# Startup of a two-block transformer kernel: loads reordered, the filter's last products moved behind the start of the first projection pass, adaLN units dealt one to three per pass

## The reference, cut to what matters

```python
mod_l = split(silu(c) @ ada_w + ada_b, 6)          # adaLN: shift, scale, gate (twice)
mod_c = split(silu(c_ctx) @ ada_w + ada_b, 6)
zc = modulate(rmsnorm(ctx, norm1_w), mod_c[0], mod_c[1]) @ w_in + b_in
zl = modulate(rmsnorm(x, norm1_w), mod_l[0], mod_l[1]) @ w_in + b_in
# hyena filter: features -> sin -> sin -> third layer, times a decay
h = sin(freq * (feats @ w1 + b1)); h = sin(freq * (h @ w2 + b2))
h = (h @ w3).reshape(L, 2, 2, 512) * exp(-t * abs(hy_decay))
kf = rfft(two_sided(h) / norm)                     # used by the hyena branch
# mLSTM branch (q, k, v, o), Fourier branch (fn), hyena branch (vh, x1, x2)
x = x + mod_l[2] * merge(gates, branches) @ w_out
x = x + mod_l[5] * hier_moe(...)
```

## Time and profile before

| | |
|---|---|
| runs | 2058.23, 2065.55, 2066.7 us; median 2065.55 |
| profiled execution | 2061.8 us, of which span 2060.0 |
| TensorE busy | 93% of the span |
| startup (to the first projection product) | 62.8 us |
| ten passes | 62.8 to 305 us |
| merge of the branches and `w_out` | to about 420 us |

### The profile page before, as it was taken

The page is one execution under the profiler, slowest core; times in us unless marked ns, Lnnn a source line. Parts: engine busy times, 40 slices in busy tenths (PEclk is TensorE's granted clock), DMA queues, the critical chain, the costliest instruction groups (busy, mean ns, idle before and its releaser), DMA issues.

```text
span 2060.0 us, 45934 instructions
## 1 busy us (share of the span) xinstructions
PE 1916.1 (93%) x20794; PEld 1295.1 (63%) x20794; DVE 663.8 (32%) x1618; ACT 295.3 (14%) x668; POOL 15.5 (1%) x25
## 2 busy tenths in 40 slices
PE   5999999998899698899997997799999999999997
PEld 2664878885795356477775555466666666666665
DVE  2656674522212455322323453301101101110123
ACT  2212121001111224100001133101000000100001
POOL 0100000000000000000000000000000000000000
PEclk7999999999899898899998998899999999999999
DMA  9856763236797422367675240499999999999995
GB/s 362 284 205 236 253 223 114 95 105 197 251 347 284 175 98 82 118 211 243 213 261 184 98 143 17 170 368 387 399 386 402 387 395 395 389 401 393 399 386 209
DMA packets 225611, 528.55 MB, mean 257 GB/s; under 512 B 14960, under 2 KB 72656, under 8 KB 225088
## 3 DMA queue, kind: packets, MB, share of 16 engines
q1 hardware_dynamic: 221168, 509.17, 67.2%
q0 software_dynamic: 1984, 8.79, 1.2%
q10 hardware_dynamic: 2256, 7.56, 1.0%
HBM read 520.49 MB, written 4.98 MB: 255 GB/s over the span
## 4 chain that ended last, share of the span: by engine, by line
PE 86%; DVE 8%; ACT 2%; DMA 2%; issue 1%; DVEq 1%; SPq 0%; ACTq 0%
PE ps L1164 26%; PE ps L1176 13%; PE ps L1120 8%; PE ps L1335 7%; PE ps L793 5%; PE ps L1102 4%; PE ps L986 4%; DVE ring L1910 3%; PE ps L1187 2%; PE ps L1001 2%; PE ps L666 2%; DMA ring<-in_ada_w 1%; PE ps L1382 1%; PE ps L688 1%; PE ps L1409 1%
## 5 line engine op out<-in xcount | busy, mean ns | idle before, releaser
L1164 PE MATMUL ps<-ring,arena 128*32 128x256 f32 (+1 forms) x10752 | 547.8, 364 | 3.8 <-DVE dn L2470 3.1
L1164 PEld LDWEIGHTS ps<-ring,arena 128*32 128x32 f32 x10752 | 364.5, 110 | 179.2 <-DVE dn L2470 3.3
L1176 PE MATMUL ps<-ring,arena 128*32 128x256 f32 x4992 | 276.0, 379 | 2.9 <-DVE arena L2527 2.9
L1176 PEld LDWEIGHTS ps<-ring,arena 128*32 128x32 f32 x4992 | 169.4, 110 | 103.4 <-issue 4.2
L1120 PE MATMUL ps<-hT,ring 128*128 128x256 f32 x704 | 158.2, 386 | 9.9 <-DMA ring<-in_w_ff_down 9.9
L2513 DVE TENSOR_TENSOR arena<-arena,ps 128x256 f32<-128x256 f32 (+1 forms) x72 | 26.9, 373 | 400.0 <-ACT arena L1720 400.0
L1335 PE MATMUL ps<-ring,hT 128*128 128x512 f32 (+1 forms) x384 | 153.6, 553 | 1.0 <-DVE hT L1939 1.0
L1120 PEld LDWEIGHTS ps<-hT,ring 128*128 128x128 f32 x704 | 135.5, 194 | 28.6 <-DMA ring<-in_w_ff_down 10.0
L1335 PEld LDWEIGHTS ps<-ring,hT 128*128 128x128 f32 x384 | 70.5, 191 | 70.2 <-issue 69.8
L1910 DVE SCALAR_TENSOR_TENSOR ring<-ring,cact 128x512 f32<-128x512 f32 x133 | 99.9, 751 | 10.3 <-issue 0.4
L793 PE MATMUL ps<-hT,ring 128*128 128x256 f32 x384 | 90.7, 390 | 2.1 <-DVE hT L1939 2.1
(11 more groups left out here) (386 smaller groups left out, 1648.7 us busy)
## 6 DMA issues: line engine op xcount, KB each, us to landing
ring<-in_w_exp_down SPq DMA_DIRECT2D x176, 512.0 KB, 7.9
ring<-in_w_exp_gate SPq DMA_DIRECT2D x128, 512.0 KB, 5.4
ring<-in_w_exp_up SPq DMA_DIRECT2D x128, 512.0 KB, 7.1
ring<-in_w_ada SPq DMA_DIRECT2D x48, 768.0 KB, 6.2
ring<-in_w_in SPq DMA_DIRECT2D x36, 768.0 KB, 7.4
ring<-in_w_exp_gate SPq DMA_DIRECT2D x64, 384.0 KB, 6.4
ring<-in_w_exp_up SPq DMA_DIRECT2D x64, 384.0 KB, 8.3
ring<-in_ada_w SPq DMA_DIRECT2D x24, 768.0 KB, 8.2
```

The source lines that it names most:

```text
L1164: last = mm(ps[32 * q:32 * q + 32, base + t_, j * n:(j + 1) * n], src[:, k, 32 * t_:32 * t_ + 32], w[:, q], start=k == 0 and j == 0, stop= ...
L1176: last = mm(ps[32 * q:32 * q + 32, bank + t_ // 2, (t_ % 2) * 256:(t_ % 2 + 1) * 256], rows[:, t_, o:o + 32], cells[:, cell, r * D + q * 2 ...
```

## The change

It does four things.

1. ScalarE's queue no longer loads ctx and the `cs`/`ss` tables; GpSimd's queue does, after the rows of units 0 to 3 (`strip_mm` 4). The decay is loaded as one row of 8 KB, and TensorE spreads it to 128 partitions: 4 products of a row of ones with 512 values each, ahead of unit 0. ScalarE takes the absolute value from PSUM. The other tables (2.3 MB) load only in the second pass.
2. The third filter layer moves into pass q: half of it after piece 0, half after piece 2. VectorE's products with the exponentials follow there, with ctx's norm between; ScalarE's exponentials come after `hT`. `turn("ctx")` waits for them. Unit 3's columns come after `turn("x1")`.
3. The adaLN units are dealt by `PASS_ADA`: one in each of the first three passes, two in v, vc and o, three in vh, x1 and x2, two in fn (before: two in each). `SUMMED` is renumbered; still seven units.
4. The filter's norms move one place back in pass k (`norm_of_filters` after piece 2), and its last step on VectorE one convolution forward.

```diff
-SUMMED = (10, 11, 12, 13, 14, 17, 19)
+PASS_ADA = (4, 5, 6, 7, 9, 11, 13, 16, 19, 22, 24)
+SUMMED = (7, 8, 9, 10, 11, 15, 18)
...
-        a, b = ADA_UNITS[4 + 2 * p:6 + 2 * p]
+        group = ADA_UNITS[PASS_ADA[p]:PASS_ADA[p + 1]]
         unit = ("in1", IN1_UNIT[name])
-        loads = loads + ([unit] if unit not in loads else []) + [a, b]
-        releases = releases + [a] + ([unit] if name not in ("k", "v") else []) + [b]
+        early = group if len(group) == 1 else group[:-1]
+        loads = loads + ([unit] if unit not in loads else []) + group
+        releases = releases + early + ([unit] if name not in ("k", "v") else []) + group[len(early):]
...
-            pool.dma_start(region(R_DEC, 2048), A["hy_decay"][0].rearrange("o d c -> (o d c)").partition_broadcast(P)
-                           ).then_inc(sem("decay_in"), 16)
-            pool.wait_ge(sem("strip_mm"), 2)
-            pool.dma_start(blob[:, NFILTER:NCONST], blob_in[:, NFILTER:NCONST]).then_inc(sem("consts_in"), 16)
-            pool.wait_ge(sem("filter_mm"), 6)
+            pool.dma_start(region(R_DEC, 2048)[0:1], A["hy_decay"].rearrange("a o d c -> a (o d c)")).then_inc(sem("decay_in"), 16)
+            pool.wait_ge(sem("strip_mm"), 4)
+            pool.dma_start(late[:, :].rearrange("p (b d) -> p b d", b=NT),
+                           A["ctx"][0].rearrange("(b p) d -> p b d", p=P)).then_inc(sem("ctx_in"), 16)
+            pool.dma_start(blob[:, NEARLY:NFILTER], blob_in[:, NEARLY:NFILTER]).then_inc(sem("spectra_tables_in"), 16)
+            pool.wait_ge(sem("filter_mm"), 7)
...
+            pool.wait_ge(sem("half_mm"), 2)
+            pool.dma_start(blob[:, NFILTER:NCONST], blob_in[:, NFILTER:NCONST]).then_inc(sem("consts_in"), 16)
...
             pe.wait_ge(sem("ident_in"), 16)
+            pe.wait_ge(sem("decay_in"), 16)
+            for j in range(4):
+                last = mm(ps[:, 4 + j, :], const("ones")[0:1, :], region(R_DEC, 2048)[0:1, j * 512:(j + 1) * 512],
+                          start=True, stop=True)
+            last.then_inc(sem("filter_mm"), 1)
...
-            strip_rows(1)
-            strip_columns(1)
-            pe.wait_ge(sem("filter_h"), 2)
-            pe.wait_ge(sem("w3_in"), 16)
-            filter_rows(0, 0, 0)
-            filter_rows(0, 1, 4)
-            strip_rows(2)
-            filter_rows(1, 0, 6)
-            strip_columns(2)
-            pe.wait_ge(sem("filter_h3"), 1)
-            filter_rows(1, 1, 0)
+            for i in (1, 2):
+                strip_rows(i)
+                strip_columns(i)
             strip_rows(3)
-            strip_columns(3)
-            pe.wait_ge(sem("filter_h3"), 3)
...
+            pe.wait_ge(sem("decay"), 1)
             turn("x1")
+            strip_columns(3)
...
+            def with_filter_rows(i):
+
+                if i == 0:
+                    pe.wait_ge(sem("filter_h"), 2)
+                    pe.wait_ge(sem("w3_in"), 16)
+                    filter_rows(0, 0, 4)
+                    filter_rows(0, 1, 6)
+                elif i == 2:
+                    pe.wait_ge(sem("filter_h3"), 2)
+                    filter_rows(1, 0, 4)
+                    filter_rows(1, 1, 6)
...
-            in_pass(0, nothing)
+            in_pass(0, with_filter_rows)
+            pe.wait_ge(sem("filter_h3"), 4)
             turn("ctx")
```

More of the change, by code:

```diff
@@ L765, in bank_free @@
                 else:
-                    pe.wait_ge(sem("filter_h3"), 4)
+                    pe.wait_ge(sem("filter_a"), 2)
             def source(p):
@@ L1552, in _ @@
             sqrt_of(1, 2, st[:, 0:2], std)
+            strip_in(1)
             act.wait_ge(sem("filter_a"), 2)
             ac(fc, fa, ACT.Sin).then_inc(sem("filter_h"), 1)
[L1555 to L1561 removed]
+            act.wait_ge(sem("filter_mm"), 2)
+            ac(region(R_DEC, 2048), all_ps[:, 2048:4096], ACT.Abs).then_inc(sem("decay"), 1)
             strip_in(2)
@@ L1589, in ml_exp @@
                 ac(w, w, ACT.Exp).then_inc(sem("ml_exp"), 1)
+            act.drain()
+            for b in range(NT):
+                ac(region(R_EXP + 2048 * b, 2048), region(R_DEC, 2048), ACT.Exp, scale=const("tneg")[:, b:b + 1]).then_inc(sem("decay"), 1)
+            act.drain()
             strip_in(4)
             z_in("q", 0)
+            sqrt_of(2, 2, st[:, 0:2], std)
+            z_in("q", 1)
+            turned(2, hTc, gac, modc)
+            strip_in(5)
             act.wait_ge(sem("filter_pq"), 1)
@@ L2052, in _, with filters_in @@
             norm_columns(1, hT, ga, mod)
+            def filters_in(b):
+                for o in range(2):
+                    bank = 4 + 2 * o
+                    dve.wait_ge(sem("filter_mm"), 4 + 2 * b + o)
+                    dve.wait_ge(sem("decay"), b + 2)
+                    v.tensor_tensor(h3[:, b, o, :, :].rearrange("p d n -> p (d n)"), ps[:, bank:bank + 2, :].rearrange("p a n -> p (a n)"),
+                                    region(R_EXP + 2048 * b + 1024 * o, 1024), ALU.mult).then_inc(sem("filter_h3"), 1)
+            filters_in(0)
+            dve.wait_ge(sem("ctx_in"), 16)
+            norm_rows(2, late[:, :].rearrange("p (b d) -> p b d", b=NT))
+            filters_in(1)
+            fence()
+            v.memset(h3[0:1, 0, :, 1, :], 0.0)
+            fence()
             for o in range(2):
@@ L2057, in _ @@
             last.then_inc(sem("filter_pq"), 1)
-            dve.wait_ge(sem("ctx_in"), 16)
-            norm_rows(2, late[:, :].rearrange("p (b d) -> p b d", b=NT))
             fence()
```

79 lines of the change are left out of this document (30 added, 49 removed).

## The result

The changed kernel took 2076.86 us (median of 8 executions, 2071.71 to 2081.99), the kernel before on the same chip 2064.77 (8 executions, 2058.23 to 2068.25): ratio 1.0066, 95% interval 1.0046 to 1.0086. It is slower by two thirds of a per cent, where 0.3% faster was forecast; the range ended at 2066. The profiled execution took 2081.2 us.

The account below looks back on a forecast made before the run. TensorE was taken as the bound, with slack only in startup waits and half clock before pass q. Terms 18.3-7.3-0.8-3.3-1.9=5.0 us gave 2056.8 from 2061.8; forecast median 2058.5, range 2050 to 2066.

Parts of the forecast that it names:

- Startup: Before pass q: fewer early loads start its first piece at 44.5 us instead of 62.76; gain 18.3, bounds 15.3 and 22.2.
- the spreading: Ahead of unit 0's rows: four decay products, 7.12 us at half clock, free if `filter` lands by 7.4 us.
- the fast bound: Startup at 2.4 GHz, bound by loads: pass q starts at 40.6 us, a gain of 22.2.
- Third layer: Third filter layer moved into pass q: costs 7.3 us at full clock, bounds 7.3 and 14.5.
- Pass v: TensorE's wait for VectorE in pass v grows from 1.6 to 2.4 us, costing 0.8.
- the sum: All terms up to the merge: 18.3-7.3-0.8-3.3-1.9=5.0 us gained, subtracted from 2061.8.
- Merge wait: Behind pass fn: merge 0, released later, lands at 313.9 us, wanted at 310.56; 3.3 us of new wait.
- slow `gates_of(0)`: Behind the merge wait: TensorE falls to half clock, costing 1.9 us, bounds 0 and 1.9.
- Whatever starts pass q earlier shifts everything after it: From pass q on: an earlier start moves all later work, because TensorE's progress releases later loads.
- Rival D: Pass q and ctx's transposes: the clock doesn't come back after the `hT` wait, 26.3 us more, 2083; chance 0.08.

Follow-up runs that it names:

- before_again: The kernel before, run once more unaltered: 2064.26 us (ratio 0.9984).
- after_two: The changed kernel with its third part undone (two units in every pass, old `SUMMED`): 2057.41 us (ratio 0.9977).
- after_shift: The changed kernel with the first piece of pass fn computed twice: 2067.84 us (ratio 0.9999).
- before_shift: The kernel before with the first piece of pass fn computed twice: 2078.28 us (ratio 1.0061).
- before_nudge: The kernel before with extra 128x256 products ahead of pass fn's first piece: six, 2076.73 us (1.0049); four, 2074.68 us (1.0036).
- after_late: The changed kernel with the first eight products of the second attention's projections computed twice: 2080.62 us (ratio 1.0070).
- after_nudge2: The changed kernel with two extra 128x256 products ahead of pass fn's first piece: 2079.46 us (ratio 1.0052).
- two_nudge6: The changed kernel with part 3 undone and six extra 128x256 products in pass fn: 2069.07 us (ratio 1.0020).
- after_att4: The changed kernel with four extra 128x256 products ahead of the second attention's third projection: 2076.12 us (ratio 1.0045).
- before_att1: The kernel before with one extra 128x256 product ahead of the second attention's third projection: 2069.48 us (ratio 1.0004).
- the fill: Unread 128x128 products in the waits of both attentions' tails; added to the changed kernel: 2066.62 us (ratio 1.0000).
- parts 1 and 2 with the fill: The changed kernel with part 3 undone, plus unread 128x128 products in the waits of both attentions' tails: 2057.89 us (ratio 0.9952).

## Why the prediction was wrong

**Startup: right, against a late base.** The first piece starts at 41.71 us against 44.5 forecast, a gain of 21.05, inside the bounds of 15.3 to 22.2. But the base of 62.76 was one execution's, the latest of five: before_again has 55.78, with 17 us at half clock where the first profile had 31. By the means of five the gain is 17.3. Unit 3's rows start at 32.29, behind a DMA wait (31.9 forecast). `filter` landed at 8.74 and not at 7, so the spreading (7.19 us, forecast 7.1) ended at 16.97 and unit 0's rows began at 16.90 instead of 15.7; the DMA waits behind absorbed that. TensorE was back at full clock for most rows between; that and the late base brought the result near the fast bound.

By the Trainium skill (DMA: Bandwidth & Descriptors, Queues, rings and completion order: each engine takes turns between queues), a queue less brings `filter` forward. It did, from 11.12 to 8.74, but by less than I took it for; no run shows the turns.

**Third layer: right.** 3.70+3.70=7.40 us at full clock, forecast 7.3. A wait of 1.07 for unit 4, on which nothing was counted, came in front.

**Pass v: right in the wait, short in the clock.** 2.48 us against 1.6 before, forecast 2.4. The columns and the spectrum behind it took 1.87+6.05 against 1.33+4.95 before: 1.6 us more that the sum left out. These terms give 21.05-7.40-1.07-0.88-1.64=10.1 where 12.40 us were measured at the end of pass fn; most of the rest is a half-clock stretch that the kernel before had at 203 us (clock 0.98 from 200 to 290 us, worth 1.8 us) and the changed kernel has not (1.00).

**Merge wait: right mechanism, too small.** 4.64 us, forecast 3.3, and 2.82 for the slow `gates_of(0)`, forecast 1.9; merge 0 is issued from 290.79 us on and lands at 302.75, 12.0 us later where 10.7 were reckoned from release to landing, while `fnet_columns` ends at 294.47+3.69=298.16. after_two shows both terms by their absence, 7.57 us. What came out larger on either side cancels: 4.78 behind the merge, forecast 5.0. That the sum met the measured pair is luck: the cancelling terms, and the base again, since the five profiles of each kernel have 0.8.

**The step that failed** is "Whatever starts pass q earlier shifts everything after it", taken to the end: the sum of 5.0 was subtracted from 2061.8 as if the identical stages behind the merge kept their durations. They didn't; 24 us were lost there in the profiled pair, of which 3.7 came without a lower clock, and by the medians some 13 (12.1 us between them and a mean lead of 0.8). The smaller failure is the base: one execution's 62.76 stood for the kernel, and the lead of 5.0 was 0.8 on average. Rival D named the right mechanism, a clock that doesn't come back, and its 2083 us was nearer than the forecast, but it sat in pass q, where the clock was 1.00 from 46 to 72 us. No row from behind 320 us went into the sum, since the change doesn't touch those stages, and so it left out that the two attentions already stood at a granted clock of 0.85 and 0.89.

**What is shown and what stays open.** Shown: that most of the loss is half-clock time in unchanged stages (stretches, rows, and the clock of every execution); that it isn't a remnant of the change (after_shift removes most of it, before_shift and the two before_nudge kernels bring a loss into the kernel before); that in the 18 profiles without a fill the long stretch goes with the place of the fall in the attention's work, though this was read off 14 of them, and 0.04 us separate the last fall with it from the first without; that with the waits filled no execution's mean clock is under 0.967, the highest of all the others. Only argued: that the place of the fall is the cause of the long stretch, and that the changed kernel's median lies high because its earlier stages bring it to the bad place oftener. Two profiles against two, and the medians, speak for it, but the forecasts by offset (after_late, after_nudge2, two_nudge6, after_att4, before_att1) failed, and I can't say which kernel will meet it. Why the changed kernel has more half-clock time than the kernel before thus stays open. Open also: whether the fill works by less idle time or because it is plain products. The tail is rich in transposes. The Trainium skill (TensorE: Matmul & The Clock Gate, Part 4) says that transposes don't count as activity in the same way; no run here separates the two. The Trainium skill (TensorE: Matmul & The Clock Gate, HAM oscillation) ties falls to single long waits between bursts. The trace has them with none longer than 1.95 us just ahead, so a long wait isn't needed for a fall here; whether several short ones are what brings it, no run separates.

## What to carry to other kernels

Where TensorE waits often between small products, its clock is on a knife's edge, and any edit upstream, even one that saves time, can tip it: look at the granted clock of all stages before costing a change, and count each stage under full clock as scatter (here 12 to 24 us on a term of 5). Take the base from several executions: one kernel's start of pass q lay anywhere from 55.8 to 62.8 us. Judge a change of a few microseconds at the row where its own work ends, over several profiles of each kernel (here 0.8 us ahead by the means of five, 4.8 in one pair), beside the total. Then take the edge away, by filling the waits with cheap products, before tuning anything by less; parts 1 and 2 with the fill gave 0.5%, the whole change without it lost 0.7%.

## What the hardware showed that I had not expected

- Profiles whose fall lies within 0.10 us of one point of the attention's work have 51 us at half clock; those farther off, from 0.14 us on, have 17 to 31. Moving the work on purpose by one product of half a microsecond did not move the median (1.0004).
- The same kernel's startup has 31 us at half clock in one execution and 17 in another, and 7 us between them behind the merge.
- The clock stayed at 0.50 over 40 us in which TensorE was busy for 32.30 with waits of up to 1.9 us and one of 4.3 at its end; the kernel before was at 0.82 in the same work (1240 to 1280 us).
- The offset between the work and the clock's changes is no free choice of the programmer: nine of eighteen profiled executions, of eight different kernels, met the second attention's tail with the fall in the same 0.17 us of its work, although that point lay anywhere from 1236.6 to 1248.9 us.
- 0.9 us of extra products in pass fn left the row behind the merge 0.1 us later than in the changed kernel, while eight products of 128x512 moved what follows them by 6.9.
